# Delta rule's triangular inversion on the diagonal 64x64 squares, multiplied on quarters of the TensorE array

## The chip, the cores and the metric

One core of one Trainium2 chip runs the whole program. The metric is the device time of the program in microseconds (us). It ran three times: 2449.15, 2449.47 and 2450.02 us, median 2449.47 us.

## The reference, cut to what matters

The program computes a whole model of four layers on one sequence of 256 tokens and width 2048: two layers that mix sliding-window attention, a convolution module and a gated delta rule, then a pooling layer and a recurrent (RG-LRU) layer. The change is in the gated delta rule alone, which runs once in each of the first two layers:

```
n = T // CHUNK                      # CHUNK = 64, T = 256, 6 heads of 128
gc = cumsum(g)                      # within a chunk
decay = exp(where(incl, gc[:, None] - gc[None, :], -inf))
kb = kc * beta
lower = where(strict, (kb @ kc.T) * decay, 0)
rhs = concat([vc * beta, kb * exp(gc)])
sol = triangular_solve(lower + eye, rhs)      # lower, unit diagonal
u, w = sol[..., :Dv], sol[..., Dv:]
# then a scan over the chunks with u, w, q, k
```

The kernel works with chunks of 128 tokens in place of 64 (the result of the recurrence is the same), so each layer has 6 heads x 2 chunks = 12 systems of 128 x 128 with a unit triangular matrix, and it forms the inverse of each.

## The kernel before, in words

All engines follow one plan of 1 MB pieces of weights ("chunks" in the code, made by `plan`). SyncE loads a piece into one of five buffers W; ScalarE rounds it to WH (L991, `high`), VectorE takes the rest W - WH into WL (L1658, `low`), and TensorE multiplies the activations with WL and WH (`Group.feed`, L454, all matmuls through the helper `mm`, L421). A piece has four slices of 128 input rows; after each slice every engine's program calls `pump`, which moves each side job (a Python generator: delta rule, conformer, attention) on by one `yield`. So the order of every engine's work is fixed in the program: a side job issues some instructions, and `yield from rest(2)` lets two slices of the main product go before its next ones. The engines meet only at semaphores (`w.wait_ge(*to(...))`). Side jobs write the upper four PSUM banks in turn (`side`, L423), which waits until the reader of that bank's last use is done.

`delta_net` exists once for each engine (TensorE L602, ScalarE L1123, VectorE L1843). The inverse is built by doubling. UU holds the inverse (upper triangular form, its 12 systems side by side, 128 columns each), TT_ its transpose, DS the strict triangle. Level 2 comes from a mask (`lv2`) and is transposed once (L628 to L634, "tu"). Then for m in LEVELS = (4, 8, 16, 32, 64, 128):

- TensorE, L661: X = DS^T TT_, 12 fp32 matmuls of 128x128 in three banks ("x"). From m = 8 on, in the same stretch (L647 to L653, `upper_of_lower`), 12 transposes of TT_ ("tr"), which ScalarE copies into UU (L1141 to L1147).
- VectorE, L1894: masks X with the table `lv{m}` into XX, three instructions of 512 columns.
- two slices of the main product later, TensorE, L670: UU^T XX, 12 fp32 matmuls ("t"; for m = 128 XX^T UU, "u"), and VectorE, L1900, adds it to TT_ (for 128 to UU).
- two slices later the next level begins.

After m = 128 the inverse is applied (L682 on, "uv" and "wk"). The profile writes a matmul's operands as moving, stationary: `PS<-TB,Q` is a transpose of Q against the identity in TB, `PS<-Q` a product of two tiles of Q, where UU, TT_, XX and DS all lie.

The attention side job, untouched, already works on parts of the array: `scores` (L770) multiplies 64 rows, with heads in turn on the lower and upper half of the rows and each in its own bank; the products with the values (L804 to L814) write 64 columns, on the lower and upper half of the columns, into one bank.

Of the kernel before, what the change touches and what calls it, by code (L numbers as in the profile page):

```python
# [106 lines left out]
def const_columns():  # L107

    i = np.arange(128)
    c = {}  # L110
    c["ident"] = np.eye(128)
    c["cum"] = i[:, None] <= i[None, :]
    c["incl"] = i[:, None] <= i[None, :]
    c["strict"] = -1.0 * (i[:, None] < i[None, :])
    up = lambda m: ((i[:, None] // m) == (i[None, :] // m)) & ((i[:, None] % m) < m // 2) & ((i[None, :] % m) >= m // 2)
    c["lv2"] = up(2)
    for m in (4, 8, 16, 32, 64, 128):
        c[f"lv{m}"] = up(m).T
# [12 lines left out]
    return {n: np.ascontiguousarray(v, dtype=np.float32) for n, v in c.items()}  # L131
# [28 lines left out]
class Signals:  # L160
# [46 lines left out]
def rest(n):  # L207

    for _ in range(n):
        yield  # L210
# [25 lines left out]
def program(nc, wall, tab, pos_d, pT_d, xin, xT_d, gpost_d, gplo_d, xsave, out):  # L236
# [6 lines left out]
    with ctx:  # L243
# [88 lines left out]
        KB, EG, DS, DI, KD = (sc(o0 + 1536 * k, 1536) for k in range(5))  # L332
        SS, VN = CK[:, 0:768], KB[:, 0:768]
        UU, TT_, XX = sc(0, 1536), sc(1536, 1536), sc(3072, 1536)
        RV, RW, U2, WT, OC = KB, CV, TT_, XX, DS
        HB = sc(16950, 1144).rearrange("p (m c) -> p m c", m=4)
        CFT = sc(16950, 1024)
# [24 lines left out]
        def hl_of(n, kt):  # L362

            return ("norm_v", n, "hl", kt | 1 if n in (1, 2) and kt < 12 else kt)

        def heads(ap):
            return ap.rearrange("p (h t c) -> p h t c", h=6, t=2)
# [47 lines left out]
        def tensor(e, w):  # L415
# [186 lines left out]
            def delta_net(l):  # L602
# [22 lines left out]
                        i.then_inc(*up("dn_p", l, which, k))  # L625
                    yield
                yield from rest(2)
                for k in range(3):  # L628
                    b = side(("dn", l, "tu", k), ("dn_a", l, "tu", k))
                    w.wait_ge(*to("dn_v", l, "uu", k))  # L630
                    for j in range(4):
                        us = slice(128 * (4 * k + j), 128 * (4 * k + j) + 128)
                        i = e.transpose(b[:, 128 * j:128 * j + 128], UU[:, us], ident)
# [11 lines left out]
                    yield from rest(2)  # L645

                def upper_of_lower(m):  # L647
                    for k in range(3):
                        b = side(("dn", l, "tr", m, k), ("dn_a", l, "u", m, k))
                        for j in range(4):  # L650
                            us = slice(128 * (4 * k + j), 128 * (4 * k + j) + 128)
                            i = e.transpose(b[:, 128 * j:128 * j + 128], TT_[:, us], ident)  # L652
                        i.then_inc(*up("dn_p", l, "tr", m, k))  # L653

                for m in LEVELS:
                    w.wait_ge(*to("dn_v", l, "kk", 2))
                    if m == 4:
                        w.wait_ge(*to("dn_a", l, "tu", 2))
                    else:
                        w.wait_ge(*to("dn_v", l, "t", m // 2, 2))  # L660
                    for k in range(3):  # L661
                        b = side(("dn", l, "x", m, k), ("dn_v", l, "x", m, k))
                        for j in range(4):
                            us = slice(128 * (4 * k + j), 128 * (4 * k + j) + 128)
                            i = mm(b[:, 128 * j:128 * j + 128], DS[:, us], TT_[:, us], start=(j == 0))
                        i.then_inc(*up("dn_p", l, "x", m, k))
                    if m > 4:
                        upper_of_lower(m // 2)
                    yield from rest(2)
                    for k in range(3):  # L670
                        w.wait_ge(*to("dn_v", l, "x", m, k))
                        if m > 4:
                            w.wait_ge(*to("dn_a", l, "u", m // 2, k))
                        which = "t" if m < 128 else "u"
                        b = side(("dn", l, which, m, k), ("dn_v", l, which, m, k))
                        for j in range(4):
                            us = slice(128 * (4 * k + j), 128 * (4 * k + j) + 128)
                            l_, r_ = (XX, UU) if which == "u" else (UU, XX)
                            i = mm(b[:, 128 * j:128 * j + 128], l_[:, us], r_[:, us], start=(j == 0))
                        i.then_inc(*up("dn_p", l, which, m, k))  # L680
                    yield from rest(2)
                w.wait_ge(*to("dn_v", l, "u", 128, 2))  # L682
# [284 lines left out]
        def scalar(e, w):  # L967
# [155 lines left out]
            def delta_net(l):  # L1123
# [11 lines left out]
                for k in range(3):  # L1135
                    w.wait_ge(*to("dn_p", l, "tu", k))
                    act(TT_[:, 512 * k:512 * k + 512], sbank("dn", l, "tu", k), ACT.Copy, "dn_a", l, "tu", k,
                        lag=k)
                yield
                yield from rest(2 * 2)  # L1140
                for m in LEVELS:  # L1141
                    yield
                    if m > 4:
                        for k in range(3):
                            w.wait_ge(*to("dn_p", l, "tr", m // 2, k))
                            act(UU[:, 512 * k:512 * k + 512], sbank("dn", l, "tr", m // 2, k), ACT.Copy,
                                "dn_a", l, "u", m // 2, k, lag=k)  # L1147
                    yield from rest(3)
                yield
                for k in range(3):  # L1150
# [453 lines left out]
        def vector(e, w):  # L1604
# [238 lines left out]
            def delta_net(l):  # L1843
# [49 lines left out]
                for m in LEVELS:  # L1893
                    for k in range(3):  # L1894
                        cs = slice(512 * k, 512 * k + 512)
                        w.wait_ge(*to("dn_p", l, "x", m, k))
                        tt(quad(XX[:, cs]), quad(sbank("dn", l, "x", m, k)),
                           tbl(f"lv{m}").unsqueeze(1).to_broadcast([128, 4, 128]), ALU.mult, "dn_v", l, "x", m, k, lag=k)
                    yield from rest(2)
                    for k in range(3):  # L1900
                        cs = slice(512 * k, 512 * k + 512)
                        which = "t" if m < 128 else "u"
                        dst = TT_ if m < 128 else UU
                        w.wait_ge(*to("dn_p", l, which, m, k))
                        tt(dst[:, cs], dst[:, cs], sbank("dn", l, which, m, k), ALU.add, "dn_v", l, which, m, k, lag=k)
# [502 lines left out]
```

## Time and profile before

| | |
|---|---|
| device time, median of 3 runs (lowest, highest) | 2449.47 us (2449.15, 2450.02) |
| the profiled execution: device time, span | 2449.32 us, 2447.5 us |
| TensorE (PE) busy | 2414.6 us, 99% of the span |
| VectorE (DVE) busy | 1657.7 us, 68% |
| ScalarE (ACT) busy | 1250.9 us, 51% |
| mean granted TensorE clock | 0.997 |
| DMA, mean | 175 GB/s |

The span is that of the first to the last instruction; 1.8 us of the device time lie outside it. The page's busy time of TensorE counts from each matmul's start to its modelled end, and ends overlap with the next starts; so lengths of stretches are better read from starts.

### The profile page before, as it was taken

Reading aid. Unit: us, or ns where it says so; the run is one execution under the profiler, and the core shown is the slowest. Engines: PE = TensorE matmul, PEld = TensorE weight load, DVE = VectorE, ACT = ScalarE, POOL = GpSimd, SP = SyncE. Lnnn points to the kernel's source line nnn. Section 1 sums busy time; section 2 is a strip of 40 time slices with the busy share of each in tenths; the row PEclk is TensorE's granted clock in tenths of the full one; section 3 lists DMA queues with packets and bytes.
Section 4 is the critical chain, followed back from the end, with each engine's and each line's share of the span. In section 5 each row is a group of like instructions: output and inputs, shape, how many; then the busy total and the mean of one; then the engine's idle time right before and its main releaser. Section 6 shows DMA issues by size and latency. Waiting matters only on the chain.

```text
span 2447.5 us, 34157 instructions
## 1 busy us (share of the span) xinstructions
PE 2414.6 (99%) x14580; PEld 2139.5 (87%) x14580; DVE 1657.7 (68%) x1895; ACT 1250.9 (51%) x1378; POOL 0.2 (0%) x4
## 2 busy tenths in 40 slices
PE   8999999999999999999999999999999999999997
PEld 8999988899999888988888888878888888888876
DVE  5788758557887585667657577565657667667764
ACT  5554256455543565544444344456556465565573
POOL 0000000000000000000000000000000000000000
PEclk9999999999999999999999999999999999999999
DMA  6543223555532335555555555555454555555553
GB/s 235 207 175 137 98 109 130 198 206 199 182 138 90 118 130 198 195 189 189 189 189 189 189 189 189 194 206 191 153 186 179 193 183 189 189 177 185 203 193 121
DMA packets 63977, 428.17 MB, mean 175 GB/s; under 512 B 7121, under 2 KB 7249, under 8 KB 14801
## 3 DMA queue, kind: packets, MB, share of 16 engines
q1 hardware_dynamic: 61280, 414.97, 47.6%
q10 hardware_dynamic: 2544, 11.01, 1.2%
q8 instruction: 115, 1.88, 0.3%
q14 instruction: 38, 0.30, 0.0%
HBM read 421.76 MB, written 4.19 MB: 174 GB/s over the span
## 4 chain that ended last, share of the span: by engine, by line
PE 97%; DVE 1%; ACT 1%; issue 0%; DMA 0%; DVEq 0%; SPq 0%; ACTq 0%
PE PS L421 95%; PE PS L547 1%; PE PS L652 1%; DVE X L1627 0%; PE PS L643 0%; PE PS L785 0%; ACT Q L977 0%; ACT WH L991 0%; PE PS L766 0%; DVE SM L1642 0%; DVE Q L1627 0%; DVE O L1623 0%; DMA W<-in_wall 0%; DVE H L1623 0%; DVE Y L1623 0%
## 5 line engine op out<-in xcount | busy, mean ns | idle before, releaser
L1658 DVE TENSOR_TENSOR WL<-W,WH 128x2048 fp32r<-128x2048 f32 (+2 forms) x392 | 860.4, 2203 | 505.7 <-ACT WH L991 505.3
L991 ACT ACTIVATE WH<-W 128x2048 fp32r<-128x2048 f32 (+2 forms) x392 | 718.0, 1842 | 506.4 <-PE PS L421 421.1
L421 PE MATMUL PS<-H,WH 128*128 128x256 f32 (+1 forms) x4864 | 946.5, 327 | 0.0
L421 PEld LDWEIGHTS PS<-H,WH 128*128 128x128 f32 x4864 | 713.0, 191 | 43.9
L421 PE MATMUL PS<-H,WL 128*128 128x256 f32 x3392 | 558.3, 284 | 7.6 <-DVE H L1627 7.6
L421 PEld LDWEIGHTS PS<-H,WL 128*128 128x128 f32 x3392 | 503.2, 190 | 50.9 <-issue 9.2
L421 PE MATMUL PS<-WH,H 128*128 128x512 f32 (+1 forms) x1280 | 331.1, 379 | 0.0
L421 PEld LDWEIGHTS PS<-WH,H 128*128 128x128 f32 x1280 | 234.1, 188 | 46.1
L421 PE MATMUL PS<-WH,YS 128*128 128x512 f32 x1024 | 273.8, 389 | 0.0
L421 PEld LDWEIGHTS PS<-WH,YS 128*128 128x128 f32 x1024 | 192.2, 188 | 40.0
L421 PE MATMUL PS<-WL,H 128*128 128x512 f32 (+1 forms) x640 | 197.2, 387 | 5.3 <-DVE H L1623 5.3
L977 ACT ACTIVATE Q<-PS 128x512 f32<-128x512 f32 (+2 forms) x142 | 75.3, 577 | 226.5 <-PE PS L421 114.2
L421 PE MATMUL PS<-WL,YS 128*128 128x512 f32 x512 | 158.0, 390 | 1.2 <-DVE YS L1623 1.2
L421 PEld LDWEIGHTS PS<-WL,H 128*128 128x128 f32 x640 | 114.8, 188 | 26.5 <-issue 7.8
L1623 DVE TENSOR_TENSOR Q<-Q,PS 128x512 f32<-128x512 f32 (+1 forms) x106 | 69.3, 680 | 88.8 <-PE PS L421 42.3
L421 PEld LDWEIGHTS PS<-WL,YS 128*128 128x128 f32 x512 | 96.0, 188 | 21.5 <-issue 1.6
L421 PE MATMUL PS<-Q 128*128 128x128 f32 (+1 forms) x960 | 112.6, 281 | 0.0
L421 PEld LDWEIGHTS PS<-Q 128*128 128x128 f32 (+1 forms) x960 | 108.9, 191 | 4.0 <-issue 1.4
L1627 DVE SCALAR_TENSOR_TENSOR QA<-Q,TB,QA 128x256 f32<-128x256 f32 x240 | 107.6, 478 | 0.0
L1627 DVE SCALAR_TENSOR_TENSOR Q<-Q,TB 128x256 f32<-128x256 f32 x206 | 93.7, 492 | 10.1 <-ACT Q L977 9.5
L977 ACT ACTIVATE Q<-Q 128x1024 f32<-128x1024 f32 (+4 forms) x58 | 65.4, 1127 | 59.1 <-DVE Q L1623 40.8
L421 PE MATMUL PS<-D,WH 128*128 128x512 f32 x256 | 69.9, 394 | 0.0
(146 smaller groups left out, 1598.9 us busy)
## 6 DMA issues: line engine op xcount, KB each, us to landing
W<-in_wall SPq DMA_DIRECT2D x374, 1024.0 KB, 4.8
W<-in_wall SPq DMA_DIRECT2D x24, 512.0 KB, 3.5
W<-in_wall SPq DMA_DIRECT2D x8, 536.0 KB, 3.6
X<-in_xT SPq DMA_DIRECT2D x8, 256.0 KB, 5.4
X<-in_x ACTq DMA_DIRECT2D x1, 2048.0 KB, 10.6
xsave<-X ACTq DMA_DIRECT2D x1, 2048.0 KB, 8.3
X<-xsave ACTq DMA_DIRECT2D x1, 2048.0 KB, 11.9
Q<-in_g_post ACTq DMA_DIRECT2D x8, 256.0 KB, 3.4
```

The lines of the kernel that those rows point to most:

```text
L421: return e.matmul(o, l, r, start=start, stop=stop, skip_group_check=True)
L547: o = e.transpose(b[:, 256 * j + 128 * t:256 * j + 128 * t + 128], X[:, t, c:c + 128], ident)
L652: i = e.transpose(b[:, 128 * j:128 * j + 128], TT_[:, us], ident)
L977: e.activation(o, a, f, **k).then_inc(*up(*sig))
L991: e.activation(WH[:, s % NSPL, 0:m], W[:, c % NRAW, 0:m], ACT.Copy).then_inc(*up("hi", c))
L1623: e.tensor_tensor(o, a, b, op).then_inc(*after(sig))
L1627: e.scalar_tensor_tensor(out=o, in0=a, scalar=s, in1=b, op0=op0, op1=op1).then_inc(*after(sig))
L1658: e.tensor_tensor(WL[:, c % NRAW, 0:m], W[:, c % NRAW, 0:m], WH[:, s % NSPL, 0:m].bitcast(F32), ALU.subtract).then_inc(*up("lo", c))
```

## The change

The inverse of a unit triangular 128x128 matrix up to m = 64 is zero outside its two diagonal 64x64 squares. The change keeps only these: TC, UC and XC are [128, 768] (rows 0 to 63 hold the upper square of each system, rows 64 to 127 the lower one) in place of TT_, UU and XX of [128, 1536], and every matmul of the levels has 64 rows, 64 columns of weights and 64 moving columns. For m = 4 (and "tu") a square of the lower rows is written to the lower output rows, one of the upper to the upper, both into the same bank. From m = 8 to 64 the two row halves write two different banks, and even and odd systems go to the lower and the upper output rows. UC is made by 12 transposes of [64 rows, 128 columns]. For m = 128 only the corner is computed: 12 matmuls for x, 12 for u, and "tr 64" is 24 matmuls against the identity, copied back into the diagonal of UU. Masks are 64 columns wide; VectorE and ScalarE handle two banks of 384 columns in place of three of 512. The number of `yield`s between the steps is the same on every engine.

```diff
-    for m in (4, 8, 16, 32, 64, 128):
-        c[f"lv{m}"] = up(m).T
+    for m in (4, 8, 16, 32, 64):
+        c[f"lv{m}"] = np.concatenate([up(m).T[0:64, 0:64]] * 2)
...
+        TC, UC, XC = TT_[:, 0:768], TT_[:, 768:1536], XX[:, 0:768]
...
+        def corner(ap, r, s):
+            return ap[64 * r:64 * r + 64, :].rearrange("p (u c) -> p u c", c=128)[:, :, 64 * s:64 * s + 64]
+        def six(ap):
+            return ap[:, 0:384].rearrange("p (u c) -> p u c", u=6)
...
-                for k in range(3):
+                lo, hi = slice(0, 64), slice(64, 128)
+                def blocks(k):
+                    for u in range(6 * k, 6 * k + 6):
+                        for r, rows in enumerate((lo, hi)):
+                            at = slice(64 * (u % 6), 64 * (u % 6) + 64)
+                            near, wide = slice(64 * u, 64 * u + 64), slice(128 * u + 64 * r, 128 * u + 64 * r + 64)
+                            yield rows, at, near, wide, u % 6 == 0
+                def by_head(r, u):
+                    c = 384 * r + 64 * (u // 2)
+                    return (lo, hi)[u % 2], slice(c, c + 64)
+                for k in range(2):
                     b = side(("dn", l, "tu", k), ("dn_a", l, "tu", k))
-                    w.wait_ge(*to("dn_v", l, "uu", k))
...
+                    w.wait_ge(*to("dn_v", l, "uu", 1 + k))
+                    for rows, at, near, wide, first in blocks(k):
+                        i = mm(b[rows, at], UU[rows, wide], ident[rows, rows], start=first)
...
                 def upper_of_lower(m):
+                        if m == 64:
+                            for rows, at, near, wide, first in blocks(k):
+                                i = mm(b[rows, at], TC[rows, near], ident[rows, rows], start=first)
+                        else:
+                            rows = (lo, hi)[k]
+                            for q in range(6):
+                                i = e.transpose(b[:, 64 * q:64 * q + 64], TC[rows, 128 * q:128 * q + 128],
+                                                ident[rows, rows])
...
+                for m in LEVELS[:-1]:
...
+                    bs = [side(("dn", l, "x", m, k), ("dn_v", l, "x", m, k)) for k in range(2)]
+                    for u in range(12):
+                        for k, rows in enumerate((lo, hi)):
+                            if m == 4:
+                                i = mm(bs[u // 6][rows, 64 * (u % 6):64 * (u % 6) + 64], DS[rows, wide],
+                                       TC[rows, near], start=(u % 6 == 0))
...
+                            else:
+                                i = mm(bs[k][(lo, hi)[u % 2], 64 * (u // 2):64 * (u // 2) + 64], DS[rows, wide],
+                                       TC[rows, near], start=(u < 2))
...
+                    for u in range(12):
+                        for r, rows in enumerate((lo, hi)):
...
+                                held, there = by_head(r, u)
+                                i = mm(bs[u % 2][rows, 64 * (u // 2):64 * (u // 2) + 64], UC[held, there],
+                                       XC[held, there], start=(u < 2))
...
+                    for u in range(6 * k, 6 * k + 6):
+                        i = mm(b[hi, 64 * (u % 6):64 * (u % 6) + 64], DS[lo, 128 * u + 64:128 * u + 128],
+                               TC[lo, 64 * u:64 * u + 64], start=(u % 6 == 0))
...
+                upper_of_lower(64)
+                yield from rest(2)
...
+                    for u in range(6 * k, 6 * k + 6):
+                        i = mm(b[lo, 64 * (u % 6):64 * (u % 6) + 64], XC[hi, 64 * u:64 * u + 64],
+                               UU[hi, 128 * u + 64:128 * u + 128], start=(u % 6 == 0))
...
+                        tt(six(XC[:, 384 * k:384 * k + 384]), six(sbank("dn", l, "x", m, k)),
+                           tbl(f"lv{m}", 64).unsqueeze(1).to_broadcast([128, 6, 64]), ALU.mult, "dn_v", l, "x", m, k,
...
+                        tt(v, v, six(sbank("dn", l, "t", m, k)), ALU.add, "dn_v", l, "t", m, k, lag=k)
```

## Rows read from the trace of the kernel before

**Rows 1.** The page: busy time of each engine, and the chain that ended last.

```profile
PE 2414.6 (99%) x14580; PEld 2139.5 (87%) x14580; DVE 1657.7 (68%) x1895; ACT 1250.9 (51%) x1378; POOL 0.2 (0%) x4
...
PE 97%; DVE 1%; ACT 1%; issue 0%; DMA 0%; DVEq 0%; SPq 0%; ACTq 0%
PE PS L421 95%; PE PS L547 1%; PE PS L652 1%; DVE X L1627 0%; PE PS L643 0%; PE PS L785 0%; ACT Q L977 0%; ACT WH L991 0%; PE PS L766 0%; DVE SM L1642 0%; DVE Q L1627 0%; DVE O L1623 0%; DMA W<-in_wall 0%; DVE H L1623 0%; DVE Y L1623 0%
```

**Rows 2.** Engines by stretch, the two inversions: busy us (instructions), clock, DMA.

```profile
248.90:321.30 72.40, 72.40 (x525) 67.36 (x524) 50.17 (x72) 21.65 (x24) 0.00 (x0) 1.00 0.25 88
741.00:813.40 72.40, 72.40 (x525) 67.35 (x525) 50.18 (x70) 21.72 (x25) 0.00 (x0) 1.00 0.25 88
```

**Rows 3.** Timeline, level 32 of layer 0 and the start of level 64.

```profile
284.80 2.84 PE L421 MATMUL PS<-Q 128*128 128x128 f32 x24
285.88 0.69 DVE L1623 TENSOR_TENSOR Q<-PS,TB 128x512 f32<-128x512 f32 x1
...
287.47 1.47 PE L652 MATMUL PS<-TB,Q 128*128 128x128 f32 x12
287.67 0.69 DVE L1623 TENSOR_TENSOR Q<-PS,TB 128x512 f32<-128x512 f32 x1 [0.20 <-PE PS L421]
288.11 1.58 ACT L977 ACTIVATE Q<-PS 128x512 f32<-128x512 f32 x3 [7.74 <-PE PS L652]
288.28 0.87 DVE L1627 SCALAR_TENSOR_TENSOR QA<-Q,TB,QA 128x256 f32<-128x256 f32 x2
...
288.70 0.71 PE L421 MATMUL PS<-WL,H 128*128 128x512 f32 x2
...
291.56 2.84 PE L421 MATMUL PS<-Q 128*128 128x128 f32 x24
292.64 0.69 DVE L1623 TENSOR_TENSOR Q<-Q,PS 128x512 f32<-128x512 f32 x1 [3.49 <-PE PS L421]
...
294.15 0.71 PE L421 MATMUL PS<-WL,H 128*128 128x512 f32 x2
...
295.83 2.28 DVE L1658 TENSOR_TENSOR WL<-W,WH 128x2048 fp32r<-128x2048 f32 x1
...
296.97 2.84 PE L421 MATMUL PS<-Q 128*128 128x128 f32 x24
```

**Rows 4.** TensorE by shape, whole span: stationary, moving, count, busy us, mean ns.

```profile
L421 PE MATMUL PS<-Q 128*128 128x128 f32 x864 | 102.5, 275 | 0.0
L421 PE MATMUL PS<-Q,TB 128*128 128x256 f32 x16 | 3.8, 378 | 0.0
L421 PEld LDWEIGHTS PS<-Q 128*128 128x128 f32 x864 | 101.5, 192 | 2.0
L421 PEld LDWEIGHTS PS<-Q 64*128 64x128 f32 x96 | 7.4, 186 | 1.9 <-issue 1.4
L421 PEld LDWEIGHTS PS<-Q,QA 128*64 128x64 f32 x144 | 8.4, 137 | 0.7 <-issue 0.7
L633 PE MATMUL PS<-TB,Q 128*128 128x128 f32 x24 | 2.9, 272 | 0.0
L652 PEld LDWEIGHTS PS<-TB,Q 128*128 128x128 f32 x120 | 13.4, 140 | 0.7 <-DVE Q L1623 0.4
```

**Rows 5.** Timeline, attention's scores on row halves, and the matmuls around them.

```profile
403.77 0.39 PE L421 MATMUL PS<-WH,YC 128*128 128x512 f32 x1
404.09 1.68 PE L421 MATMUL PS<-Q 64*128 64x128 f32 x16
405.71 0.50 PE L421 MATMUL PS<-WL,YC 128*128 128x512 f32 x1
```

**Rows 6.** Timeline, attention's values on column halves.

```profile
437.58 4.42 PE L421 MATMUL PS<-Q,QA 128*64 128x128 f32 x72
```

**Rows 7.** Timeline of 390.90 to 390.94: the first two loads of a scores stretch.

```profile
390.91 0.20 PEld L421 LDWEIGHTS PS<-Q 64*128 64x128 f32 x2
```

**Rows 8.** VectorE by shape: columns, count, busy us, mean ns.

```profile
L1623 DVE TENSOR_TENSOR Q<-PS,TB 128x512 f32<-128x512 f32 x36 | 24.1, 688 | 3.4 <-PE PS L421 3.2
L1623 DVE TENSOR_TENSOR Q<-PS,SM 128x256 f32<-128x256 f32 x12 | 4.2, 418 | 0.2
```

**Rows 9.** The list of waits within 248.9 to 321.3: us in total, times, longest.

```profile
ACT Q L977 <- PE PS L652: 39.7, 5, 8.1
DVE Q L1623 <- PE PS L421: 22.0, 26, 3.5
ACT WH L991 <- PE PS L421: 10.2, 4, 7.9
ACT QA L977 <- PE PS L421: 0.7, 1, 0.7
PEld PS L652 <- DVE Q L1623: 0.2, 1, 0.2
```

More of the change, by code:

```diff
@@ L627, in delta_net @@
                 yield from rest(2)
-                for k in range(3):
+                lo, hi = slice(0, 64), slice(64, 128)
[9 more added lines that the diff above has]
+                for k in range(2):
                     b = side(("dn", l, "tu", k), ("dn_a", l, "tu", k))
-                    w.wait_ge(*to("dn_v", l, "uu", k))
-                    for j in range(4):
-                        us = slice(128 * (4 * k + j), 128 * (4 * k + j) + 128)
-                        i = e.transpose(b[:, 128 * j:128 * j + 128], UU[:, us], ident)
+                    w.wait_ge(*to("dn_v", l, "uu", 1 + k))
+                    for rows, at, near, wide, first in blocks(k):
+                        i = mm(b[rows, at], UU[rows, wide], ident[rows, rows], start=first)
                     i.then_inc(*up("dn_p", l, "tu", k))
@@ L647, in upper_of_lower @@
                 def upper_of_lower(m):
-                    for k in range(3):
+                    for k in range(2):
                         b = side(("dn", l, "tr", m, k), ("dn_a", l, "u", m, k))
-                        for j in range(4):
-                            us = slice(128 * (4 * k + j), 128 * (4 * k + j) + 128)
-                            i = e.transpose(b[:, 128 * j:128 * j + 128], TT_[:, us], ident)
+                        if m == 64:
[6 more added lines that the diff above has]
+                                                ident[rows, rows])
@@ L653, in upper_of_lower @@
                         i.then_inc(*up("dn_p", l, "tr", m, k))
-                for m in LEVELS:
+                for m in LEVELS[:-1]:
                     w.wait_ge(*to("dn_v", l, "kk", 2))
                     if m == 4:
-                        w.wait_ge(*to("dn_a", l, "tu", 2))
+                        w.wait_ge(*to("dn_a", l, "tu", 1))
                     else:
[L660 to L666, printed above, removed]
+                        w.wait_ge(*to("dn_v", l, "t", m // 2, 1))
+                    bs = [side(("dn", l, "x", m, k), ("dn_v", l, "x", m, k)) for k in range(2)]
+                    for u in range(12):
+                        for k, rows in enumerate((lo, hi)):
+                            near, wide = slice(64 * u, 64 * u + 64), slice(128 * u + 64 * k, 128 * u + 64 * k + 64)
+                            if m == 4:
+                                i = mm(bs[u // 6][rows, 64 * (u % 6):64 * (u % 6) + 64], DS[rows, wide],
+                                       TC[rows, near], start=(u % 6 == 0))
+                                if u % 6 == 5 and k == 1:
+                                    i.then_inc(*up("dn_p", l, "x", m, u // 6))
+                            else:
+                                i = mm(bs[k][(lo, hi)[u % 2], 64 * (u // 2):64 * (u // 2) + 64], DS[rows, wide],
+                                       TC[rows, near], start=(u < 2))
+                                if u == 11:
+                                    i.then_inc(*up("dn_p", l, "x", m, k))
@@ L669, in delta_net @@
                     yield from rest(2)
[L670 to L680, printed above, removed]
@@ L681, in delta_net @@
-                    yield from rest(2)
-                w.wait_ge(*to("dn_v", l, "u", 128, 2))
+                    w.wait_ge(*to("dn_v", l, "x", m, 1))
+                    if m > 4:
+                        w.wait_ge(*to("dn_a", l, "u", m // 2, 1))
+                    bs = [side(("dn", l, "t", m, k), ("dn_v", l, "t", m, k)) for k in range(2)]
+                    for u in range(12):
+                        for r, rows in enumerate((lo, hi)):
+                            if m == 4:
+                                i = mm(bs[u // 6][rows, 64 * (u % 6):64 * (u % 6) + 64],
+                                       UU[rows, 128 * u + 64 * r:128 * u + 64 * r + 64],
+                                       XC[rows, 64 * u:64 * u + 64], start=(u % 6 == 0))
+                                if u % 6 == 5 and r == 1:
+                                    i.then_inc(*up("dn_p", l, "t", m, u // 6))
+                            else:
+                                held, there = by_head(r, u)
+                                i = mm(bs[u % 2][rows, 64 * (u // 2):64 * (u // 2) + 64], UC[held, there],
+                                       XC[held, there], start=(u < 2))
+                                if u > 9 and r == 1:
+                                    i.then_inc(*up("dn_p", l, "t", m, u % 2))
@@ new lines, in delta_net @@
+                    yield from rest(2)
+                w.wait_ge(*to("dn_v", l, "t", 64, 1))
+                for k in range(2):
+                    b = side(("dn", l, "x", 128, k), ("dn_v", l, "x", 128, k))
+                    for u in range(6 * k, 6 * k + 6):
+                        i = mm(b[hi, 64 * (u % 6):64 * (u % 6) + 64], DS[lo, 128 * u + 64:128 * u + 128],
+                               TC[lo, 64 * u:64 * u + 64], start=(u % 6 == 0))
+                    i.then_inc(*up("dn_p", l, "x", 128, k))
@@ new lines, in delta_net @@
+                upper_of_lower(64)
+                yield from rest(2)
+                for k in range(2):
+                    w.wait_ge(*to("dn_v", l, "x", 128, k))
+                    w.wait_ge(*to("dn_a", l, "u", 64, k))
+                    b = side(("dn", l, "u", 128, k), ("dn_v", l, "u", 128, k))
+                    for u in range(6 * k, 6 * k + 6):
+                        i = mm(b[lo, 64 * (u % 6):64 * (u % 6) + 64], XC[hi, 64 * u:64 * u + 64],
+                               UU[hi, 128 * u + 64:128 * u + 128], start=(u % 6 == 0))
+                    i.then_inc(*up("dn_p", l, "u", 128, k))
@@ L683, in delta_net @@
+                yield from rest(2)
+                w.wait_ge(*to("dn_v", l, "u", 128, 1))
                 for k in range(3):
@@ L1134, in delta_net @@
                 yield from rest(11 + 7 + 4)
-                for k in range(3):
+                for k in range(2):
                     w.wait_ge(*to("dn_p", l, "tu", k))
-                    act(TT_[:, 512 * k:512 * k + 512], sbank("dn", l, "tu", k), ACT.Copy, "dn_a", l, "tu", k,
+                    act(TC[:, 384 * k:384 * k + 384], sbank("dn", l, "tu", k)[:, 0:384], ACT.Copy, "dn_a", l, "tu", k,
                         lag=k)
@@ L1142, in delta_net @@
                     yield
-                    if m > 4:
-                        for k in range(3):
+                    if 4 < m < 128:
+                        for k in range(2):
                             w.wait_ge(*to("dn_p", l, "tr", m // 2, k))
-                            act(UU[:, 512 * k:512 * k + 512], sbank("dn", l, "tr", m // 2, k), ACT.Copy,
+                            act(UC[:, 384 * k:384 * k + 384], sbank("dn", l, "tr", m // 2, k)[:, 0:384], ACT.Copy,
                                 "dn_a", l, "u", m // 2, k, lag=k)
+                    if m == 128:
+                        for k in range(2):
+                            w.wait_ge(*to("dn_p", l, "tr", 64, k))
+                            for r in range(2):
+                                act(corner(UU, r, r)[:, 6 * k:6 * k + 6, :],
+                                    six(sbank("dn", l, "tr", 64, k)[64 * r:64 * r + 64, :]), ACT.Copy,
+                                    *(("dn_a", l, "u", 64, k) if r else ()), lag=2 * k + r)
                     yield from rest(3)
@@ L1892, in delta_net @@
                 yield from rest(2)
-                for m in LEVELS:
-                    for k in range(3):
-                        cs = slice(512 * k, 512 * k + 512)
+                for m in LEVELS[:-1]:
+                    for k in range(2):
                         w.wait_ge(*to("dn_p", l, "x", m, k))
-                        tt(quad(XX[:, cs]), quad(sbank("dn", l, "x", m, k)),
-                           tbl(f"lv{m}").unsqueeze(1).to_broadcast([128, 4, 128]), ALU.mult, "dn_v", l, "x", m, k, lag=k)
+                        tt(six(XC[:, 384 * k:384 * k + 384]), six(sbank("dn", l, "x", m, k)),
+                           tbl(f"lv{m}", 64).unsqueeze(1).to_broadcast([128, 6, 64]), ALU.mult, "dn_v", l, "x", m, k,
+                           lag=k)
                     yield from rest(2)
[L1900 to L1905, printed above, removed]
-                    yield from rest(2)
+                    for k in range(2):
+                        if m > 4:
+                            v = TC.rearrange("p (q two c) -> p q two c", q=6, two=2)[:, :, k, :]
+                        else:
+                            v = six(TC[:, 384 * k:384 * k + 384])
+                        w.wait_ge(*to("dn_p", l, "t", m, k))
+                        tt(v, v, six(sbank("dn", l, "t", m, k)), ALU.add, "dn_v", l, "t", m, k, lag=k)
+                    yield from rest(2)
+                for k in range(2):
+                    w.wait_ge(*to("dn_p", l, "x", 128, k))
+                    copy(XC[64:128, 384 * k:384 * k + 384], sbank("dn", l, "x", 128, k)[64:128, 0:384],
+                         "dn_v", l, "x", 128, k, lag=k)
+                yield from rest(2)
+                for k in range(2):
+                    w.wait_ge(*to("dn_p", l, "u", 128, k))
+                    copy(corner(UU, 0, 1)[:, 6 * k:6 * k + 6, :], six(sbank("dn", l, "u", 128, k)[0:64, :]),
+                         "dn_v", l, "u", 128, k, lag=k)
+                yield from rest(2)
                 yield from rest(6)
```

## Prediction

> **What bounds the kernel now.** I read the page first: TensorE is busy 99% of the span and carries 97% of the chain that ended last, nearly all through the matmul helper [rows 1]. The reader is to see that no other engine sets the end anywhere for long. Then the two inversions by stretch: in 72.4 us each, TensorE has no gap at all at full clock, VectorE is busy 50 us, ScalarE 22 us, and DMA moves only 88 GB/s [rows 2]. The list of waits of that stretch has the other engines waiting for TensorE, 73 us in all, and TensorE once for 0.2 us [rows 9]. So every microsecond that TensorE saves there should come off the end, until a wait turns around. Last the timeline of one level [rows 3], for its pieces.
>
> **What the removed work costs.** One fp32 product appears in the trace as two pairs of a weight load and a matmul (24 records for 12 products). The 24 records last 2.84 us with the last one's latency of 0.275 [rows 3, 4]; so a pair costs (2.84 - 0.275) / 23 = 0.1115 us, and a stretch of 12 products 24 x 0.1115 = 2.68 us. The 12 transposes are single pairs: (1.47 - 0.272) / 11 = 0.109 each, 1.31 us a stretch; 0.272 is the latency of these records [rows 4]. A level from x to the next x lasts 296.97 - 284.80 = 12.17 us, of which 2 x 2.68 + 1.31 = 6.67 are the inversion and 5.50 four slices of the main product.
> In each layer: "tu" 1.31, twelve x, t or u stretches 32.16, five "tr" 6.55: **40.0 us**.
>
> **What a 64x64 product costs.** Two rows give the price of a pair on one tile. A load of 64 weight columns takes 137 ns where 128 take 192, so 55 ns less; a matmul of 256 moving columns takes 378 where 128 take 275, 0.8 ns per column, so 64 columns stream in some 52 [rows 4]. Load and matmul overlap now, so a pair on one tile takes 54.5 ns, half of 109. The same would be true without any working side by side; then the new form would win nothing, because it has more products.
> Whether tiles work side by side is seen in attention. The values: 72 pairs with 64 weight columns and 128 moving columns start within 4.42 - 0.27 = 4.15 us, 58 ns apart, though each takes 109 on its tile [rows 6]; 4.26 us against 3.92 for two perfect halves. The scores: 8 pairs with 128 and 8 with 256 moving columns would take 8 x 0.109 + 8 x 0.217 = 2.61 us on the full array (0.217 is 256 columns at that rate); they take 1.68 - 0.38 + 0.22 = 1.52 [rows 5]. And the other row half's first load starts 0.01 us after the first, although six instructions of the first head lie between them in the program (two loads of 0.19 cover 0.20) [rows 4, 7]. So both row halves and column halves run side by side, and the queue looks some instructions ahead.
>
> - Two tiles in turn (diagonal quarters: "tu", x4, t4, "tr 64"): 24 products, 48 pairs, 24 x 0.0545 = 1.31 us.
> - One tile only (x128, u128): 12 products, 24 pairs, also 1.31 us.
> - Four quarters (x and t of m = 8 to 64): between 12 x 0.0545 = 0.65 us with four and 1.31 with two at work. Nothing in the trace has four. A product is four instructions, and a look-ahead of the size seen in rows 7 covers about two products, so I take the middle, 1.0.
> - 12 transposes of 64 rows, six on each half one after the other: loads of transposes are short (140 ns), the moving part 64 columns, so 0.65 us in sequence, 0.33 side by side; I take 0.5.
>
> **The switches.** A matmul on the full array, one on halves, and one on quarters do not overlap. From 403.77 to 405.71 there are 1.94 us; the matmul at 403.77 takes its 0.23 of streaming, and the one at 405.71 is 0.11 longer than its like (0.50 against 0.39), so the scores stretch costs 1.82 in the main stream [rows 5]. Its matmuls stream for some 1.42 of it (1.52 less the first load). That leaves 0.40 for going in and out: **0.2 us a switch**. Each layer gets 13 tiled stretches ("tu", ten of m = 4 to 64, two of 128): 26 switches, and in four of them a further one from quarters to the 64x128 transposes: 30 switches, 6.0 us. This is new work, and it is on the path. The bounds are 0.15 (a shorter load of 64 columns goes first) and 0.25.
>
> **Sum for each layer.** "tu", x4, t4: 3 x 1.31 = 3.93. Eight x and t: 8.0. Four "tr": 2.0. x128, "tr 64", u128: 3.93. Together 17.9, with switches **23.9 us** against 40.0: 16.1 us less, 32.3 us for both layers. A level of 12.17 us should become 5.50 + 3.5 = 9.0. The profiled execution took 2449.3 us, 0.15 below the median of the runs; 2449.3 - 32.3 = **2417.0 us**.
>
> **What I cost at nothing, and its cover.** VectorE's instructions go from three of 0.69 us to two of 384 columns, by interpolation 0.55 [rows 8]: it becomes lighter by 36 x 0.69 - 24 x 0.55 = 12 of its 50 us, in a stretch that shrinks by 16. Between the end of an x and the start of its t lie two slices, 2.75 us by the half of 5.50. After the last matmul's signal (0.20 us late [rows 3]) VectorE needs 2 x 0.55 = 1.1: 1.3 of 2.75. Before, it could begin on the first bank while the second was made; now the two banks of m = 8 to 64 end together, which the cover bears. ScalarE's copies, 0.5 each, begin after "tr" and end 1.3 us later. The four half copies into UU at m = 128 take under 2 us, also inside. The weights' halves (ScalarE's WH, VectorE's WL) are made three pieces ahead. The smaller tables of masks and the later start of "tu" (it waits for the second third of UU, which VectorE has long made) cost nothing that shows. The ring of side banks has two uses per step in place of three, so the one short wait of "tr" for VectorE goes, 0.2 us [rows 9].
>
> **Rivals.**
> B, one tile at a time. If the sequencer starts a pair only every 54.6 ns, as in the densest stretch of this trace (the values' two halves start a pair every 109 / 2 [rows 6]), quarters do not help: 312 products are 624 pairs, with 48 transposes 672; 672 x 0.0546 = 36.7, plus 6.0, makes 42.7 us against 40.0. Two layers: **2454.7 us, slower**. It decides once a pair costs over (40.0 - 6.0) / 672 = 50.6 ns. For it: no row shows a denser start over many pairs. Against: the 54.6 is just what two tiles of 109 give, and the two loads of rows 7 start 13 ns apart or less. The same time comes out if the 64x64 form does not engage tiles at all. The Trainium skill ("TensorE: Matmul & The Clock Gate", section "Wait — 56ns, not 53.3ns?") has a floor of this kind, 62 ns a matmul where the sequencer's firmware decodes it, and 25 ns else; an estimate by 25 would make the four-quarter stretches 1.2 us in place of 1.0 and the time 2420, one by 62 gives 2465. The 58 ns of rows 6 lie under the 62, though a full queue could hide it.
> C, two row halves cannot write one bank. "tu", x4, t4 and "tr 64" do that; then each costs 2.62 in place of 1.31, 5.2 us a layer: **2427.5 us**. Against: they write different output rows. The column halves that share a bank [rows 6] read the same rows, so they don't settle it. The Trainium skill ("TensorEngine Tiling (Array Packing)", Restrictions and Gotchas) says that different row tiles cannot access the same bank at once; no run here shows it so far, and its rule speaks against the diagonal quarters alone.
> D, VectorE is late. If its 2.28 us WL and 0.87 us of taps [rows 3] stand before the masks, t must wait 0.2 + 3.15 + 1.1 - 2.75 = 1.7 us. At half of the 12 hand-overs in both layers: 12 x 1.7 = 20 us back, **2437 us**. For it: fewer TensorE microseconds for the same WL and taps. Against: VectorE had 22 us of waiting for TensorE there [rows 9].
>
> **Chances and range.** Mine 0.66 (with its bounds: quarters 0.65 to 1.31, switches 0.15 to 0.25, transposes 0.33 to 0.65, that is 2407 to 2426), C 0.10, D 0.07, B 0.14, the rest 0.03. About 0.2%, 5 us, can be told from no change. Faster: mine, C and D, 0.83. Slower: B, 0.14. Within: 0.03. The range from 2407 to 2436 takes in mine, C and most of D and leaves B and the rest out.
>
> **What would show it.** Right: levels of about 9 us; 1248 matmul records of 64*64 whose starts in the x and t of m = 8 to 64 are some 20 ns apart, in the diagonal stretches 27; a hole of 0.2 us at each change of tile size; TensorE still without waits for VectorE. B: starts never closer than 50 ns. C: 54 ns in the diagonal stretches only. D: "PE waits for DVE" in the list of waits. The forecast is wrong if the switch costs over 0.7 us, since 60 switches then eat the gain.

## The result, and the profile after

The changed kernel takes **2410.86 us** (median of 4 runs, 2410.26 to 2411.02) where the kernel before took 2449.56 beside it (4 runs): a ratio of 0.9842, 95% interval 0.9827 to 0.9858, 38.7 us less. A second set of runs gave 2410.09 against 2449.05, the same ratio. The forecast was 2417.0, in a range from 2407 to 2436. The mechanism came as forecast; the gain is 6 us larger.

Level 32 of layer 0, which stands before in [rows 3], by the timeline of the changed kernel (TensorE, VectorE and ScalarE in order of time):

```profile
276.30 0.93 PE L429 MATMUL PS<-Q 64*64 64x64 f32 x48
277.16 0.77 PE L677 MATMUL PS<-TB,Q 64*128 64x64 f32 x12
277.39 1.01 DVE L1689 TENSOR_TENSOR Q<-PS,TB 128x384 f32<-128x384 f32 x2
277.78 0.87 ACT L1036 ACTIVATE Q<-PS 128x384 f32<-128x384 f32 x2 [4.48 <-PE PS L677]
277.85 0.73 PE L429 MATMUL PS<-WL,H 128*128 128x512 f32 x2
...
280.80 0.93 PE L429 MATMUL PS<-Q 64*64 64x64 f32 x48
281.66 0.73 PE L429 MATMUL PS<-WL,H 128*128 128x512 f32 x2
281.76 1.02 DVE L1689 TENSOR_TENSOR Q<-Q,PS 128x384 f32<-128x384 f32 x2 [2.57 <-PE PS L429]
...
284.60 0.29 PE L429 MATMUL PS<-Q 64*64 64x64 f32 x4
```

The level lasts 284.60 - 276.30 = 8.30 us in place of 12.17. An x or t stretch has twice the records (48 pairs), and its starts span little over a quarter of the time, 0.71 us in place of 2.57: (0.93 - 0.22) / 47 = 0.015 us on average from start to start, where the full array needed 0.1115 (0.22 is the length of one record). How so many start is seen in the first 0.03 us of the stretch (same columns; weight loads, then matmuls):

```profile
276.30 0.15 PEld L429 LDWEIGHTS PS<-Q 64*64 64x64 f32 x4 [0.35 <-issue]
276.30 0.29 PE L429 MATMUL PS<-Q 64*64 64x64 f32 x4
```

And by shape over the whole span (count, busy us, mean ns):

```profile
L429 PE MATMUL PS<-Q 64*64 64x64 f32 x1056 | 27.7, 222 | 0.0
L429 PE MATMUL PS<-TB,Q 64*64 64x64 f32 x192 | 6.5, 220 | 0.0
L429 PEld LDWEIGHTS PS<-Q 64*64 64x64 f32 x1056 | 24.4, 134 | 7.1 <-issue 6.4
```

The records number 1056 + 192 = 1248, as forecast. Four loads of 0.13 us each lie within 0.15: all four quarters have begun. The single records of the trace go on in this way: four matmuls start 5 to 8 ns apart, one group every 58 ns, so 15 ns is an average. The 0.35 in brackets is the time without a weight load at the change of array size. It is not all lost: the last matmul of the main product still streams its 512 columns in it, some 0.2 us.

The diagonal stretches, two quarters, and the last corner product, one quarter, and m = 128, by the timeline of a second profile of the same kernel (the first of the runs below):

```profile
249.62 1.62 PE L429 MATMUL PS<-Q 64*64 64x64 f32 x48
254.23 1.61 PE L429 MATMUL PS<-Q 64*64 64x64 f32 x48
258.84 0.93 PE L429 MATMUL PS<-Q 64*64 64x64 f32 x48
...
292.14 1.43 PE L429 MATMUL PS<-Q 64*64 64x64 f32 x21
...
297.87 1.61 PE L429 MATMUL PS<-Q 64*64 64x64 f32 x24
...
302.26 0.49 PE L429 MATMUL PS<-Q 128*128 128x128 f32 x3
```

48 pairs on two quarters and 24 pairs on one take the same 1.6 us. On one quarter a pair so takes (1.61 - 0.22 - 0.05) / 23 = 0.058 us; 0.05 is what the first pair waits for its weights (its record lasts 0.27 us, the later ones 0.22). From 292.14 to 302.26 is all of m = 128: 10.12 us.

The list of waits of the stretch from x4 to the end of the inversion (248.9 to 304.0), the one that answers to [rows 9]:

```profile
ACT Q L1036 <- PE PS L677: 19.1, 4, 5.4
DVE Q L1689 <- PE PS L429: 10.6, 6, 2.7
ACT WH L1050 <- PE PS L429: 9.8, 4, 6.9
ACT Q L1036 <- PE PS L429: 5.3, 1, 5.3
DVE Q L1704 <- PE PS L429: 3.5, 1, 3.5
PEld PS L429 <- issue: 3.2, 9, 0.4
ACT QA L1036 <- PE PS L429: 0.3, 1, 0.3
```

TensorE waits for no engine; its only entry is "issue", nine of the pauses of the weight loads at changes of size. The others wait for it 49 us in these 55.1 us, where it was 73 in 72.4. On the page TensorE is still busy 99% of the span and holds 97% of the chain:

```profile
PE 2375.8 (99%) x15204; PEld 2093.1 (87%) x15204; DVE 1633.6 (68%) x1871; ACT 1244.1 (52%) x1370; POOL 0.2 (0%) x4
...
PE 97%; DVE 1%; ACT 1%; issue 0%; DMA 0%; DVEq 0%; SPq 0%; ACTq 0%
```

TensorE's busy time is 38.8 us less than in [rows 1], the device time 38.7 less: all of the saving comes off the end. Clock (0.997) and the main product are as before.

### The profile page after: what moved, and what is told of

Read it like the earlier page. It is cut to its first block, busy times and chain, and to the rows that moved or that the text cites. A ratio compares the mean times of both kernels' runs of the same rounds, so it can differ in the third digit from the quotient of the medians.

```text
span 2409.2 us, 35375 instructions
## 1 busy us (share of the span) xinstructions
PE 2375.8 (99%) x15204; PEld 2093.1 (87%) x15204; DVE 1633.6 (68%) x1871; ACT 1244.1 (52%) x1370; POOL 0.2 (0%) x4
## 4 chain that ended last, share of the span: by engine, by line
PE 97%; DVE 1%; ACT 1%; issue 0%; DMA 0%; DVEq 0%; SPq 0%; ACTq 0%
PE PS L429 96%; PE PS L555 1%; DVE X L1693 0%; PE PS L677 0%; PE PS L664 0%; PE PS L844 0%; ACT Q L1036 0%; ACT WH L1050 0%; PE PS L825 0%; DVE SM L1708 0%; DMA W<-in_wall 0%; DVE Q L1693 0%; DVE O L1689 0%; DVE H L1689 0%; DVE Y L1689 0%
## 5 line engine op out<-in xcount | busy, mean ns | idle before, releaser
L1036 ACT ACTIVATE Q<-PS 128x512 f32<-128x512 f32 (+3 forms) x134 | 68.9, 553 | 195.5 <-PE PS L429 125.3
L1689 DVE TENSOR_TENSOR Q<-Q,PS 128x512 f32<-128x512 f32 (+1 forms) x90 | 54.9, 649 | 69.1 <-ACT Q L1036 38.2
L429 PEld LDWEIGHTS PS<-Q 64*64 64x64 f32 (+2 forms) x1440 | 65.8, 149 | 9.7 <-issue 7.8
L429 PE MATMUL PS<-Q 64*64 64x64 f32 (+2 forms) x1440 | 72.2, 240 | 0.0
```

The source lines that it names most:

```text
L1689: e.tensor_tensor(o, a, b, op).then_inc(*after(sig))
```

## Experiments

The first four and the next four kernels were each compared in one set of runs, with the kernel before beside them at 2449.05 us both times; the last two have it at 2449.38.

**The changed kernel again.** No edit.

> The changed kernel as it is, for the comparison on the same chip. Expected: about 2411 us, levels 8 to 64 of 8.3 us each, four quarters at work (one load and matmul pair started every 15 ns within an x or t stretch).

Measured: 2410.09 us (ratio 0.9842, 0.9825 to 0.9858). The measure for the next runs.

**Two quarters in turn in place of four.** Only the order of the loops for m = 8 to 64 (written out here as loops; in the kernel two functions list this order):

```diff
-for u in range(12):
-    for k, rows in enumerate((lo, hi)):          # x
+for k in range(2):
+    for u in range(12):
...
-for u in range(12):
-    for r in range(2):                           # t
+for p in range(2):
+    for u in range(p, 12, 2):
+        for r in range(2):
```

> The same products, banks and signals for m = 8 to 64, but all products with the lower 64 input rows first, then all with the upper ones, so that only two quarters stand next to each other in the program. Theory (quarters run side by side only within a short look-ahead of the queue): each of the 16 x and t stretches grows from 0.71 to about 1.38 us of starts, together +10.7 us, 2422 us. Rival 1 (the queue sorts tiles over the whole stretch of 96 instructions): no change, 2411. Rival 2 (the gain is the halved work, not the working side by side): no change, 2411.

Measured: 2418.83 us (0.9875, 0.9861 to 0.9890), +8.7. The timeline of one x stretch and its transposes:

```profile
276.44 1.44 PE L429 MATMUL PS<-Q 64*64 64x64 f32 x48
277.81 0.77 PE L687 MATMUL PS<-TB,Q 64*128 64x64 f32 x12
```

The starts span 1.44 - 0.22 = 1.22 us in place of 0.71, in 16 stretches 8.2 us. Both rivals, which wanted no change, fall. The growth is 0.51 a stretch, less than the 0.67 expected: six pairs overlap where the order changes from one half to the other. By the single records the third and the fourth quarter start at 276.97, 6 ns apart, when 18 of the first 24 pairs have started, so that three are left on each of the first two quarters.

**One quarter at a time.** The loops once more, six products of a quarter in a row (written out as above):

```diff
-for u in range(12):
-    for k, rows in enumerate((lo, hi)):          # x
+for k in range(2):
+    for p in range(2):
+        for u in range(p, 12, 2):
...
+for p in range(2):                               # t
+    for r in range(2):
+        for u in range(p, 12, 2):
```

> The same again, but the six products of one quarter stand together, 24 instructions, before the next quarter's. Theory: one quarter works at a time, 48 pairs of 58 ns, 2.78 us in place of 0.71 in 16 stretches, +33 us, about 2444 us: nearly the whole gain is lost, a little less where two quarters overlap at each change. Rival 1 (free sorting) and rival 2 (halved work alone): no change, 2411.

Measured: 2435.94 us (0.9945, 0.9930 to 0.9960), +25.9 where +33 was expected.

```profile
282.99 2.47 PE L429 MATMUL PS<-Q 64*64 64x64 f32 x48
285.40 0.76 PE L687 MATMUL PS<-TB,Q 64*128 64x64 f32 x12
```

The starts span 2.25 us, 1.54 more than 0.71; 16 x 1.54 = 24.7. A quarter alone would need 47 x 0.058 = 2.7 us. The 0.5 us that are missing are the overlaps at the three places where the quarter changes: three pairs each, 9 x 0.058. The second quarter starts at 283.51, when nine of the first one's twelve pairs have started. So another quarter's pair starts when three pairs of the one in work are left. In the order before there were six pairs left in all, three on each quarter; in these two orders the look-ahead goes by the pairs that wait for one quarter, not by the number of instructions between. The same products in the same sizes thus cost 2411 or 2436 us by their order alone: two thirds of the 38.7 us hang on it. What is left, 13 us against the kernel before, comes in about equal parts from the other stretches, where nothing was reordered (before 13.3 us a layer, now 9.8), and from the levels 8 to 64, which are still 3 us a layer shorter: the overlaps and the shorter transposes outweigh the switches there.

**Transposes as products.** In four levels the 12 transposes become 24 products with the identity on four quarters:

```diff
-rows = (lo, hi)[k]
-for q in range(6):
-    i = e.transpose(b[:, 64 * q:64 * q + 64], TC[rows, 128 * q:128 * q + 128], ident[rows, rows])
+for u in range(12):
+    for k, rows in enumerate((lo, hi)):
+        i = mm(bs[k][(lo, hi)[u % 2], 64 * (u // 2):64 * (u // 2) + 64],
+               TC[rows, 64 * u:64 * u + 64], ident[rows, rows], start=(u < 2))
...
```

> The 12 transposes of 64 rows and 128 columns in four levels replaced by 24 products with the identity on the four quarters: 48 pairs in place of 12, no change of tile size within the stretch, and 96 pairs in a row in one tile size. Theory (a pair every 14.6 ns as long as four quarters alternate): the transposes with their switch cost 0.69 us a level now, 48 pairs cost 0.70: no change, 2411 within 0.5. Rival (the dense stretch lives on instructions that the queue had collected before, and runs dry): the second 48 pairs come at 30 to 60 ns, 1.4 to 2.9 us in place of 0.7, in 8 stretches +6 to +18 us.

Measured: 2410.52 us (0.9843, 0.9828 to 0.9858): no change.

```profile
283.21 0.93 PE L429 MATMUL PS<-Q 64*64 64x64 f32 x48
283.96 0.88 PE L429 MATMUL PS<-TB,Q 64*64 64x64 f32 x48
```

96 pairs start without a hole at the same pace: the second 48 begin 0.75 us after the first and their busy time is 0.88. So at 96 pairs in a row the pace still holds.

**More changes of size.** The first six transposes move into the middle of the x products:

```diff
+                        if m > 4 and u == 5:
+                            upper_of_lower(m // 2, (0,))
                     if m > 4:
-                        upper_of_lower(m // 2)
+                        upper_of_lower(m // 2, (1,))
```

> The same products and transposes, but in four levels the six transposes of the lower row half stand in the middle of the x products in place of behind them: three changes of tile size inside the stretch in place of one, 16 more in both layers. Theory (a change of tile size costs 0.15 us of TensorE): +2.4 us and some tenths for the side by side work lost at the cuts, 2412.5 to 2414 us. Rival (the price of a stretch is in going from and to the main product only): no change, 2410.

Measured: 2414.71 us (0.9860, 0.9846 to 0.9873), +4.6, somewhat over the expected.

```profile
276.36 0.58 PE L429 MATMUL PS<-Q 64*64 64x64 f32 x24
276.87 0.59 PE L677 MATMUL PS<-TB,Q 64*128 64x64 f32 x6
277.39 0.58 PE L429 MATMUL PS<-Q 64*64 64x64 f32 x24
277.90 0.58 PE L677 MATMUL PS<-TB,Q 64*128 64x64 f32 x6
278.41 0.72 PE L429 MATMUL PS<-WL,H 128*128 128x512 f32 x2
```

From the start of x to the main product 2.05 us in place of 1.55: 0.50 more in eight stretches, 4.0 us. The first x part's last pair starts at 276.36 + 0.58 - 0.22 = 276.72 and streams for 0.06; the transposes start at 276.87 and their first waits 0.05 for its weights: 276.92 - 276.78 = **0.14 us a change of size**. Two more make 0.28; the other 0.2 is what the two halves of the transposes take longer, as they no longer overlap. From the main product into a stretch the same working gives 0.14 too; from a stretch back to the main product it gives 0.2 (level 32 of the changed kernel: the last pair of t starts at 281.51 and streams for 0.06, the main product starts at 281.66 and waits 0.11 for its weights). So a change within the stretch costs as one into it, and the rival falls.

**Masks twice and four times.** VectorE repeats the mask of each x bank for m = 8 to 64:

```diff
+                        for _ in range(1 if m > 4 else 0):       # 3 in the second kernel
+                            tt(six(XC[:, 384 * k:384 * k + 384]), six(sbank("dn", l, "x", m, k)), ...
```

> VectorE does each mask of m = 8 to 64 twice, 1.0 us more before each t, 8 times. Theory (two slices of the main product and the transposes, 3.45 us from the end of x to t, cover 0.2 + 2.1 us of VectorE): no change, 2410 within 0.6. Rival (VectorE has come next to the critical path, as its share of the stretch rose): +4 to +8 us, 2414 to 2418.

> The same masks four times, 3.1 us more before each t. Theory: VectorE now needs 0.2 + 4.1 us where 3.45 are covered, so t waits about 0.85 us in 8 stretches: +7 us, 2417, with VectorE as what TensorE waits for in the list of waits. Rival (the cover is much longer than two slices): no change.

Measured: 2411.79 us (0.9848, 0.9834 to 0.9861) and 2425.82 us (0.9904, 0.9891 to 0.9918). Twice is +1.7, above the expected 0.6: in each layer one stretch, the t of level 16, waits 0.4 us. That is 0.9 of the 1.7; the rest has no wait that shows and is within the spread of this kernel's runs (2411.01 to 2412.45). Four times is +15.7, twice the expected 7. The timeline of that t shows why, first with the masks twice:

```profile
271.55 0.93 PE L429 MATMUL PS<-Q 64*64 64x64 f32 x48 [0.36 <-DVE Q L1689]
```

Then four times, with VectorE's rows before it:

```profile
268.48 2.28 DVE L1724 TENSOR_TENSOR WL<-W,WH 128x2048 fp32r<-128x2048 f32 x1
...
270.68 4.76 DVE L1689 TENSOR_TENSOR Q<-PS,TB 128x384 f32<-128x384 f32 x8
...
275.50 0.69 PE L429 MATMUL PS<-Q 64*64 64x64 f32 x32 [2.73 <-DVE Q L1689]
```

In this level the WL instruction of 2.28 us stands in front of the masks, as rival D had it: they begin 2.5 us after the start of their x stretch (268.20), where level 32 of the changed kernel has 1.1. In the other three levels of the layer t waits 1.2 to 1.3 us by the profile. By the distances from x to t the four levels are 6.8 us longer, 13.6 in both layers. A repeated mask also cost 0.60, not 0.53; the edit makes each of these masks wait for the one before. What was added less what t then waited is the slack left in the changed kernel: 2.40 - 1.01 - 0.43 = 1.0 us in level 16 (2.40 is the length of its masks made twice, 0.43 the growth from x to t), and from 4.76 - 1.01 - 1.4 = 2.3 to 2.5 in the others. The changed kernel's own timeline agrees: its masks end 1.0 us before t starts in level 16, and 278.40 to 280.80, 2.4 us, before it in level 32.

**Packed ends.** Three edits of the changed kernel: at m = 128 corner and transposing products alternate, the last product uses both output halves, and the first transposes ("tu") go back to the full array:

```diff
-for u in range(6 * k, 6 * k + 6):
-    i = mm(b[hi, ...], DS[lo, 128 * u + 64:128 * u + 128], TC[lo, 64 * u:64 * u + 64], start=(u % 6 == 0))
...
-upper_of_lower(64)
+for rows, at, near, wide, first in blocks(k):
+    i2 = mm(b2[rows, at], TC[rows, near], ident[rows, rows], start=first)
+    if rows is lo:
+        i = mm(b[hi, at], DS[lo, wide.start + 64:wide.stop + 64], TC[lo, near], start=first)
...
+for u in range(12):
+    i = mm(b[(lo, hi)[u % 2], 64 * (u // 2):64 * (u // 2) + 64], XC[hi, 64 * u:64 * u + 64],
+           UU[hi, 128 * u + 64:128 * u + 128], start=(u < 2))
...
-    for rows, at, near, wide, first in blocks(k):
-        i = mm(b[rows, at], UU[rows, wide], ident[rows, rows], start=first)
+    i = e.transpose(b[:, 128 * j:128 * j + 128], UU[:, us], ident)       # tu, and ScalarE: 6 copies for 2
```

> Three edits of the changed kernel that should beat it: at m = 128 the corner's products (one quarter) and the transposing products (two quarters) alternate in the program, so three quarters work side by side, 1.4 us in place of 2.8; the last corner product uses both output halves, 0.7 in place of 1.4; the first transposes go back to the full array, 1.31 in place of 1.73 with its two switches. Theory: 2 x (1.4 + 0.7 + 0.4) = 5.0 us less, 2405 us. Rival (other waits, the copies of ScalarE at m = 128 or the first copies in six pieces, take it back): 2408 to 2411.

Measured: 2407.71 us (0.9832, 0.9818 to 0.9845), 2.4 under the changed kernel, not 5. A row that the changed kernel does not have tells where the rest went:

```profile
245.54 1.25 PE L665 MATMUL PS<-TB,Q 128*128 128x128 f32 x8 [0.44 <-DVE Q L1694]
```

The transposes of k wait for VectorE. So the third edit was taken out, and tried alone.

> Of the three edits of the packed ends only the two at m = 128. Theory (there the profile shows 1.9 us a layer less from x128 to the next products, and the edit of the first transposes gives its saving back): -3.8 us against the changed kernel, 2406.3 us, under the packed ends' 2407.7. Rival (the edit of the first transposes does save its 0.8 us and the rest was misjudged elsewhere): 2408.5.

> Of the three edits only the first transposes on the full array, with six short copies on ScalarE in place of two. Theory (the copies take 2.4 us of ScalarE in place of 1.0, WH and with it WL come later, and the transposes of k wait for VectorE): 0 to +1.5 us against the changed kernel, 2410 to 2411.5, with TensorE waiting for VectorE at the k transposes. Rival: -0.8 us, 2409.3.

Measured: **2406.50 us** (0.9823, 0.9810 to 0.9837) with the two edits at m = 128 alone, and 2411.64 us (0.9845, 0.9831 to 0.9858) with the third alone. Against the kernel before in their set, 42.9 and 37.7 us less, where the changed kernel has 38.7 to 39.0: the first two edits win 4, the third loses about 1. The timeline of m = 128 with the two edits:

```profile
292.50 0.27 PE L429 MATMUL PS<-TB,Q 64*64 64x64 f32 x1
292.50 0.27 PE L429 MATMUL PS<-Q 64*64 64x64 f32 x1
...
297.00 0.91 PE L429 MATMUL PS<-Q 64*64 64x64 f32 x24
...
300.70 0.49 PE L429 MATMUL PS<-Q 128*128 128x128 f32 x3
```

8.20 us in place of 10.12, 3.8 for both layers. And of the third edit alone, the list of waits from 236 to 250:

```profile
PEld PS L665 <- DVE Q L1693: 0.8, 2, 0.7
ACT WH L1051 <- PE PS L429: 0.8, 1, 0.8
DVE WL L1728 <- ACT WH L1051: 0.6, 1, 0.6
```

VectorE now waits 0.6 us for WH, which ScalarE makes after six short copies, and TensorE waits for VectorE: the stretch of the k transposes lasts 2.04 us from start to the next start (244.72 to 246.76) where the changed kernel has 1.22. So the edit pays 0.8 us a layer for the 0.4 that it saves, which is the loss of about 1 us in both layers. That the copies are what delays WH fits their length (2.4 us against two of 0.49) and the start of WH (240.85 in place of 240.13), but a kernel with the copies alone was not run.

## Why the prediction was right, and where its size was off

Its steps against the trace, for each layer:

| step | forecast, us | measured, us |
|---|---|---|
| removed (before) | 40.0 | 40.0 |
| "tu", x4, t4 with their switches | 3 x 1.71 | 3 x 1.73 |
| levels 8 to 64, four times | 3.5 | 8.30 - 5.50 = 2.80 |
| m = 128 | 4.73 | 10.12 - 5.50 = 4.62 |
| sum | 23.9 | 21.0 |

Measured 1.73 is 254.23 - 249.62 = 4.61 less two slices of 12 matmuls at 0.12. Twice 40.0 - 21.0 is 38.0 us, of 38.7 measured; the forecast had 32.3. **The term that was mis-sized is the level 8 to 64**, by 0.7 us, eight times, 5.6 of the missing 6.4:

- The four quarters. The step took "about two products" of look-ahead and the middle, 1.0 us. The starts span 0.71, with the last pair 0.77: all four quarters work. What the runs show is that the next quarter starts once three pairs are left on each quarter in work. That is enough when each quarter's turn is two pairs long, gives two quarters when the order offers two, and little when it is twelve long. The bound of 0.65 was the right end. Two stretches, 0.5 us a level. The three pairs stood in the trace before: by the code seven instructions, not the six that the prediction counts, lie between the two loads of [rows 7], the rest of one pair and three more.
- The switch. 0.14, below the low bound, for three of a level's five (into x, from x to the transposes, into t), and 0.2, as forecast, for the two back to the main product: 0.8 us in place of 1.0. The load in front has 64 or 128 columns here; in the scores it has 128.
- The transposes took 0.77 - 0.22 + 0.06 = 0.6 in place of 0.5. The three together are 0.6 of the 0.7.

**Rivals.** B (a pair only every 54.6 ns) is refuted by the first stretch: 15 ns. Its price went by 54.6 ns a pair, where [rows 6] give 4.15 / 71 = 58; with 58.5 it would be 672 x 0.0585 + 6.0 = 45.3 us a layer, 2460. On one quarter a pair does take 58 ns, but two and four quarters share that time. The order with one quarter at a time, nearest to B in these 16 stretches, stands at 2436 and not at B's 2454.7, since the other stretches kept their order and three pairs overlap at each change. C (two row halves cannot write one bank) is refuted: x4 and t4 do that, with 48 pairs in 1.6 us, the pace of two quarters, 29 ns. The rule of the Trainium skill that spoke for C, in "TensorEngine Tiling (Array Packing)", Restrictions and Gotchas, does not hold in that width for outputs on different rows: the two row halves write one bank at the same pace as if each were alone. The Trainium skill's "PSUM — Partial Sum Buffer" (section "PSUM bank collisions raise a hardware error"), which quotes the wide rule too, reports the conflict between row tiles for the same bank and the same 32 rows of it, and the 29 ns agree with that. D (VectorE late) did not happen, but the repeated masks show how near it is: 1.0 us more of VectorE in front of t, and it begins in level 16. The forecast of 2.75 us of cover left out that the transposes add 0.7 to it and that in level 16 WL, standing first, takes 1.4 away. The 0.20 us that it read from [rows 3] as the delay of a signal is VectorE's idle time before its third mask; in the changed kernel VectorE starts 0.16 us after the last x matmul ends.

The floor of 25 ns from start to start that the Trainium skill gives in "TensorE: Matmul & The Clock Gate" (section "Wait — 56ns, not 53.3ns?") does not hold here either: 48 matmuls on four quarters start 15 ns apart on average, and 5 to 8 ns apart within a group of four; on one quarter they start 58 apart.

## What to carry to other kernels

Small products on quarters of the array worked side by side here only when the program alternated the quarters closely: two (load, matmul) pairs of one, then the next. The order alone was worth 26 us. A change of array size cost 0.14 us on the way in and 0.2 on the way back, so gather products of one size, and let a stretch with a free quarter take in independent work (two edits at m = 128 won another 4 us). And before a step is moved back to its cheaper form on the bound engine, count the instructions it adds to the engines that feed it.

## What the runs showed of the hardware that was not expected

Four quarters, with two row halves writing two banks, run at the full pace of four, 15 ns a pair on average, and 96 pairs in a row keep that pace. A quarter's own pace is 58 ns for a load of 64 columns and 64 moving fp32 columns, and it is the same alone, with one neighbour, or with three (24, 48 and 48 pairs in 1.6, 1.6 and 0.93 us). A new quarter starts when three pairs are left on each quarter in work, in an order with one at a time and in one with two; so matmuls of different quarters do not start in the order of the program.
